# Experts share a job of 128 rows on TensorE's column tiles, and their rows are summed to tokens on chip

## The reference, cut to what matters

```python
def moe_ffn(h, ...):                          # h: (264, 1024)
    ...                                       # sigmoid scores, 4 of 8 groups, top 8 of 64 experts
    gates = jnp.zeros((n, N_EXPERTS)).at[rows, idx].set(w)
    hg = jnp.einsum('nd,edf->nef', h, e_gate)         # e_gate, e_up: (64, 1024, 256)
    hu = jnp.einsum('nd,edf->nef', h, e_up)
    act = jax.nn.silu(hg) * hu * gates[:, :, None]
    routed = jnp.einsum('nef,efd->nd', act, e_down)   # e_down: (64, 256, 1024)
    return routed + shared                            # then x = x + gate2 * this, and a final rmsnorm
```

## Time and profile before

| | |
|---|---|
| median of 3 runs | 1032.44 us (1031.85 to 1032.86) |
| profiled execution, time | 1032.33 us |
| profiled execution, span | 1030.6 us |
| TensorE busy | 935.5 us (91% of the span) |
| VectorE, ScalarE, GpSimd busy | 474.7, 282.3, 174.7 us |
| moved by DMA | 305.58 MB, mean 297 GB/s |
| HBM read, written | 304.78 MB, 26.97 MB |

### The profile page before, as it was taken

The page is one execution under the profiler, slowest core; times in us unless marked ns, Lnnn a source line. Parts: engine busy times, 40 slices in busy tenths (PEclk is TensorE's granted clock), DMA queues, the critical chain, the costliest instruction groups (busy, mean ns, idle before and its releaser), DMA issues.

```text
span 1030.6 us, 18438 instructions
## 1 busy us (share of the span) xinstructions
PE 935.5 (91%) x6425; PEld 653.2 (63%) x6425; DVE 474.7 (46%) x1210; ACT 282.3 (27%) x501; POOL 174.7 (17%) x173
## 2 busy tenths in 40 slices
PE   2799999999998988999998988989989999999980
PEld 1699999999997876445555545545545554555540
DVE  1556899899858443622233223223223322322217
ACT  3544435434373220111212112112111211211232
POOL 2000000000000001022223213213223222322322
PEclk9899999999999969999999999989999999999995
DMA  9975558777766185589999999999999999999922
GB/s 333 266 232 150 181 167 287 245 248 289 240 228 235 54 340 219 188 300 331 359 366 377 396 347 371 367 337 377 392 363 381 402 387 370 391 395 388 373 77 108
DMA packets 103497, 305.58 MB, mean 297 GB/s; under 512 B 13251, under 2 KB 55363, under 8 KB 78452
## 3 DMA queue, kind: packets, MB, share of 16 engines
q1 hardware_dynamic: 89715, 283.80, 73.4%
q0 software_dynamic: 13232, 19.68, 7.9%
q10 hardware_dynamic: 499, 1.40, 0.4%
HBM read 304.78 MB, written 26.97 MB: 322 GB/s over the span
## 4 chain that ended last, share of the span: by engine, by line
PE 63%; DMA 29%; DVE 5%; ACT 1%; issue 1%; SPq 1%; ACTq 0%; DVEq 0%; POOLq 0%
DMA wexp<-in_e_up 27%; PE psum L755 25%; PE psum L1022 14%; PE psum L759 5%; PE psum L1024 4%; PE psum L1050 3%; PE psum L1055 2%; PE psum L774 2%; PE psum L945 2%; DMA bc<-in_norm_g 1%; PE psum L810 1%; PE psum L1025 1%; PE psum L936 1%; PE psum L993 1%; DVE wexp_r L1436 1%
## 5 line engine op out<-in xcount | busy, mean ns | idle before, releaser
L755 PE MATMUL psum<-xn_r,wexp_r 128*128 128x264 f32 x1024 | 192.6, 288 | 2.2 <-DVE wexp_r L1436 2.2
L1024 PE MATMUL psum<-wexp,mid 128*64 128x256 f32 x720 | 173.9, 384 | 0.6 <-DMA wexp<-in_e_up 0.6
L1025 PE MATMUL psum<-wexp,mid 128*64 128x256 f32 x720 | 174.0, 384 | 0.0
L1022 PE MATMUL psum<-wexp,mid 128*128 128x512 f32 x304 | 149.3, 637 | 24.2 <-DMA wexp<-in_e_up 23.4
L755 PEld LDWEIGHTS psum<-xn_r,wexp_r 128*128 128x128 f32 x1024 | 161.0, 191 | 4.9 <-DVE wexp_r L1436 2.7
L1840 DVE SCALAR_TENSOR_TENSOR hT<-psum,gcol,hT 128x256 f32<-128x256 f32 (+1 forms) x64 | 30.6, 478 | 288.0 <-ACT hT L1347 221.3
L755 PE MATMUL psum<-hT_r,wexp_r 128*128 128x264 f32 x512 | 146.0, 285 | 0.0
L1436 DVE TENSOR_TENSOR wexp_r<-wexp,wexp_r 128x1024 fp32r<-128x1024 f32 x88 | 106.4, 1216 | 27.5 <-ACT wexp_r L1189 27.2
L1024 PEld LDWEIGHTS psum<-wexp,mid 128*64 128x64 f32 x720 | 92.3, 136 | 39.2 <-issue 6.1
L1022 PEld LDWEIGHTS psum<-wexp,mid 128*128 128x128 f32 x304 | 58.9, 204 | 86.5 <-issue 85.4
L1189 ACT ACTIVATE wexp_r<-wexp 128x1024 fp32r<-128x1024 f32 x88 | 92.1, 1053 | 49.3 <-PE psum L755 42.5
(11 more groups left out here) (287 smaller groups left out, 1119.4 us busy)
## 6 DMA issues: line engine op xcount, KB each, us to landing
wexp<-in_e_gate SPq DMA_DIRECT2D x64, 1024.0 KB
wexp<-in_e_up SPq DMA_DIRECT2D x64, 1024.0 KB
wexp<-in_e_down SPq DMA_DIRECT2D x64, 1024.0 KB
wexp<-in_w_in SPq DMA_DIRECT2D x32, 1024.0 KB, 6.0
mid<-in_ada_w SPq DMA_DIRECT2D x8, 2048.0 KB, 9.7
wexp<-in_ada_w SPq DMA_DIRECT2D x4, 2048.0 KB, 20.2
wexp<-in_w_branch SPq DMA_DIRECT2D x8, 1024.0 KB, 5.1
wexp<-in_w_out SPq DMA_DIRECT2D x4, 1024.0 KB, 5.8
```

What stands on the lines that cost most here:

```text
L755: last = mm(out, a[x], b[y], start=start and x == y == 0, stop=stop and x == 1)
L1022: last = mm(psum[:, j % 2, :].rearrange("p (a f) -> p a f", a=2), x[:, k, :], w[:, k], start=(k == 0), stop=(k == KT - 1))
L1024: mm(psum[HALF:CAP, j % 2, 0:FE], x[:, k, 0:HALF], w[:, k, 0], start=(k == 0), stop=(k == KT - 1), tile_position=(0, HALF))
L1025: last = mm(psum[0:HALF, j % 2, 0:FE], x[:, k, 0:HALF], w[:, k, 1], start=(k == 0), stop=(k == KT - 1), tile_position=(0, 0))
```

## The change

- Jobs: 33 in place of 64. Body 0 is as before (four jobs, one expert each). Seven bodies follow with eight experts each: jobs 0 and 1 have one expert (up to 128 rows), job 2 two (64 rows each), job 3 four (32 rows each). A last job has four. The rows of a job's experts stand side by side in its 128 rows; `up` and `down` run one product per expert on its column tile (64 or 32 wide), each with 512 columns streaming.
- Rooms: there are still four. Job 0 uses room 0, job 1 room 1, job 2 rooms 2 and 3, job 3 all four, and SyncE's order of loads is written anew.
- Sums: no scatter and no tables in DRAM. `down`'s result is split into a high part (ScalarE) and a low part (VectorE), and two steps later TensorE multiplies a one-hot of tokens (`spread_hot`, 128 rows by 264 tokens) by both parts in five pieces (`sum_piece`): four of 128 tokens x 512 columns in the one-pass format, and one for the 8 samples in f32 on two column tiles. VectorE adds each piece to `y_sum` in SBUF. The pieces stand between the parts of `up`, which is cut in four.
- Gathers take 128 rows for each job. The lists of a shared job are sums over its experts (up to 12 small products). The end of the kernel reads `y_sum` in place of the tables, and VectorE does all of it.

```diff
+BODIES = 7
+LAST = BODIES + 1
+N_JOBS = UNROLL * LAST + 1
+PER_BODY = 8
+SHARE = (1, 1, 2, 4)
+FIRST_PLACE = (0, 1, 2, 4)
+SINGLES = 2 * BODIES
+PAIRED = 2 * BODIES
...
+        y_sum = mod_room[:, 0:2 * D].rearrange("p (t d) -> p t d", t=2)
+        y_sum_samples = mod_room[0:SAMPLE_ROWS, 2 * D:2 * D + BLK]
...
-        y_rows = mT[:, :, :].rearrange("p k t -> p (k t)")[:, 0:2 * D].rearrange("p (b d) -> p b d", b=2)
+        y_high, y_low = [mT[:, :, :].rearrange("p k t -> p (k t)")[:, a * D:(a + 1) * D] for a in range(2)]
...
+        def share_of(i, j):
+
+            if isinstance(i, int) and i in (0, LAST):
+                return 4 if i else 1
+            return SHARE[j]
...
+        def rooms_of(i, j):
+
+            share = share_of(i, j)
+            return [j] if share == 1 else [2, 3] if share == 2 else [0, 1, 2, 3]
+
+        def loads_until(i, j):
+
+            if isinstance(i, int) and i == 0:
+                return 1
+            return 2 * i + (1 if j == 3 else 0)
+
+        def parts_of(i, j):
+
+            n = P // share_of(i, j)
+            return [(q, room, slice(q * n, (q + 1) * n), {} if n == P else {"tile_position": (0, q * n)})
+                    for q, room in enumerate(rooms_of(i, j))]
...
-            def reload(i, s):
-                n = UNROLL * i + s
-                e = expert_of(i, s)
-                sp.wait_ge(S["up_done"], n - 3)
-                load_gate_up(e, s)
-                pi, ps = (i if s else i - 1), (s - 1) % UNROLL
-                if isinstance(pi, int) and pi == 0:
-                    return
-                before = expert_of(pi, ps)
-                sp.wait_ge(S["down_done"], 2 * (n - 4))
-                load_down(before, ps)
...
+            def jobs_before(i, j, room):
+
+                if j == 3:
+                    return UNROLL * i + min(room, 2) + 1
+                if isinstance(i, int) and i == 1:
+                    return room + 1
+                return UNROLL * i
+
+            def gate_up_of(i, j):
+                for place, room in zip(places_of(i, j), rooms_of(i, j)):
+                    e = expert_at(place)
+                    sp.wait_ge(S["up_done"], jobs_before(i, j, room))
+                    load_gate_up(e, room)
+
+            def down_of(i, j):
+                for place, room in zip(places_of(i, j), rooms_of(i, j)):
+                    e = expert_at(place)
+                    sp.wait_ge(S["down_done"], 2 * jobs_before(i, j, room))
+                    load_down(e, room)
+
+            def body(i):
+                gate_up_of(i, 0)
+                if isinstance(i, int) and i == 1:
+                    sp.wait_ge(S["shared_done"], 6)
+                    load_down(1, 1)
+                gate_up_of(i, 1)
+                down_of(i, 0)
+                gate_up_of(i, 2)
+                down_of(i, 1)
+                gate_up_of(i, 3)
+                down_of(i, 2)
+                down_of(i, 3)
...
+            body(1)
+            with sp.Fori(2, LAST) as i:
+                body(i)
+            gate_up_of(LAST, 0)
+            down_of(LAST, 0)
...
-            def scatter(i, j):
-                e = UNROLL * i + j
-                pool.wait_ge(S["scatter_row_ready"], e + 1)
-                need(pool, scattered[j % 2], 16 * (2 * i + j // 2))
-                pool.wait_ge(S["ys_act"], e + 1)
-                pool.wait_ge(S["ys_dve"], e + 1)
...
-                g.indirect_dma_start(out=(y_even, y_odd)[j % 2], out_offset=bass.IndirectOffsetOnAxis(ap=scatter_row[0:n, j, :].bitcast(mybir.dt.uint32), axis=0),
-                                     in_=y_rows[0:n, j % 2, :], in_offset=None,
-                                     bounds_check=last_token, oob_is_err=False, compute_op=ALU.add).then_inc(scattered[j % 2], 16)
...
                 for k in ks:
-                    if is_large(i, j):
-                        last = mm(psum[:, j % 2, :].rearrange("p (a f) -> p a f", a=2), x[:, k, :], w[:, k], start=(k == 0), stop=(k == KT - 1))
-                    else:
-                        mm(psum[HALF:CAP, j % 2, 0:FE], x[:, k, 0:HALF], w[:, k, 0], start=(k == 0), stop=(k == KT - 1), tile_position=(0, HALF))
-                        last = mm(psum[0:HALF, j % 2, 0:FE], x[:, k, 0:HALF], w[:, k, 1], start=(k == 0), stop=(k == KT - 1), tile_position=(0, 0))
+                    for q, room, rows, tile in parts_of(i, j):
+                        last = mm(psum[rows, j % 2, :].rearrange("p (a f) -> p a f", a=2), x[:, k, rows], w_gu[room][:, k],
...
+                need(pe, S["y_lo_rows"], 2 * e)
+                need(pe, S["sum_done"], N_PIECES * e)
...
+                for h in range(2):
+                    for f in range(2):
+                        for q, room, rows, tile in parts_of(i, j):
+                            last = mm(psum[rows, 3 + h, :], a[:, f, rows], w_dn[room][:, f, h * BLK:(h + 1) * BLK],
+                                      start=(f == 0), stop=(f == 1), **tile)
+                    last.then_inc(S["down_done"], 1)
...
+            def sum_piece(hot, m):
+
+                t, h, bank = piece_of(m)
+                t0, n = TILES[t]
+                if t < 2:
+                    for y in (y_high, y_low):
+                        last = mm(psum[:, bank, :], as_r(hot[:, t0:t0 + n]), as_r(y[:, h * BLK:(h + 1) * BLK]), start=(y is y_high), stop=(y is y_low))
+                    return last
+                for y in (y_high, y_low):
+                    for h in range(2):
+                        last = mm(psum[32 * h:32 * h + n, bank, :], as_r(hot[:, t0:t0 + n]).bitcast(F32), as_r(y[:, h * BLK:(h + 1) * BLK]).bitcast(F32),
+                                  start=(y is y_high), stop=(y is y_low), tile_position=(0, 32 * h))
+                return last
+
+            def sums(i, j, pieces):
+
+                e = UNROLL * i + j
+                for m in pieces:
+                    if m == 0:
+                        pe.wait_ge(S["hot_ready"], e + 1)
+                        pe.wait_ge(S["y_lo_rows"], 2 * e + 2)
+                    else:
+                        need(pe, S["sum_done"], N_PIECES * e + m - 1)
+                    sum_piece(spread_hot[:, j % 2], m).then_inc(S["sum_full"], 1)
...
-            def body(i, first=False, last=False):
-                for j in range(UNROLL):
+            def body(i, first=False):
+                for j in steps(i):
                     prev = not (first and j == 0)
                     pi, pj = (i if j else i - 1), (j - 1) % UNROLL
-                    up(i, j, (0, 1, 2, 3))
+                    older = two_before(i, j)
+                    done = not (first and j < 2)
+                    up(i, j, (0, 1))
+                    if done:
+                        sums(*older, (0, 1))
+                    up(i, j, (2, 3))
                     if prev:
                         if first and j == 1:
                             pe.wait_ge(S["job_ready"], 1)
                         turn_act(pi, pj)
                     else:
                         turn_for_sort()
-                    up(i, j, (4, 5, 6, 7))
-                    if not (last and j == UNROLL - 1):
+                    if done:
+                        sums(*older, (2, 3))
+                    up(i, j, (4, 5))
+                    if done:
+                        sums(*older, (4,))
+                    up(i, j, (6, 7))
+                    if not (isinstance(i, int) and i == LAST):
...
-                need(ac, scattered[j % 2], 16 * (2 * i + j // 2))
-                F(y_rows[0:n, j % 2, 0:BLK], psum[CAP - n:CAP, 3, :], ACT.Copy).then_inc(S["ys_act"], 1)
-
+                need(ac, S["sum_full"], N_PIECES * e)
+                for h in range(2):
+                    ac.wait_ge(S["down_done"], 2 * e + h + 1)
+                    F(as_r(y_high[:, h * BLK:(h + 1) * BLK]), psum[:, 3 + h, :], ACT.Copy).then_inc(S["y_hi_rows"], 1)
...
+            def spread_out_rows(i, j):
 
                 e = UNROLL * i + j
                 ve.wait_ge(S["lst_ready"], e + 1)
-                need(ve, scattered[j % 2], 16 * (2 * i + j // 2 - 1))
-                n = rows_used(i, j)
-                V.tensor_copy(scatter_row[0:n, j, :], idx[0:n, j, :]).then_inc(S["scatter_row_ready"], 1)
+                need(ve, S["sum_full"], N_PIECES * (e - 1))
+                if isinstance(e, int) and e == 0:
+                    ve.wait_ge(S["tokens_ready"], 1)
+                V.tensor_scalar(as_r(spread_hot[:, j % 2, :]), token_order, token_of[:, j, :], None, ALU.is_equal).then_inc(S["hot_ready"], 1)
+
+            def add_piece(m, done):
+
+                t, h, bank = piece_of(m)
+                to = y_sum[:, t, h * BLK:(h + 1) * BLK] if t < 2 else y_sum_samples
+                n = P if t < 2 else SAMPLE_ROWS
+                V.tensor_tensor(to, psum[0:n, bank, :], to, ALU.add).then_inc(done, 1)
+
+            def sums_out(i, j):
+
+                e = UNROLL * i + j
+                need(ve, S["sum_done"], N_PIECES * e)
```

(68 more changed lines are left out.)

317 lines of the change are left out of this document (150 added, 167 removed).

## The result

The changed kernel takes 1187.24 us (median of 4 runs, 1182.87 to 1192.56), the one before 1032.65 us beside it (4 runs): a ratio of 1.149, 95% interval 1.145 to 1.153. The forecast was 1148 us in a range of 1110 to 1190, so the sign and the range held. The time is 39 us above the likeliest value and outside the narrower own range of 1125 to 1175. The profiled execution took 1184.55 us for a span of 1182.7.

What follows compares the result with a forecast made beforehand. Waits from SyncE's load order were to bound it, with TensorE idle some 20 us a body. Body 1 ends at 537.1, six bodies of 86.9 reach 1058.5, last quad and tail 1146, plus 1.7: 1148 us; range 1110 to 1190.

Steps and rivals of the forecast that it cites:

- The long wait: Before a body's first up, TensorE idles some 12 us until room 0's gate/up weights land.
- the one before the quad: TensorE waits about 8 us before the quad's up, for gate/up of rooms 2 and 3.
- the first term: From the end of a quad's up to the next body's first up: 4.3 + 3.0 + 2 x 2.44 + 4.9 = 17.0 us.
- first step with the clock: A body's first single: a step of 15.6 us, plus 1.9 us for slow records after the wait.
- second step: A body's second single: 15.6 us, from 11.8 + 1.9 + 1.7 + 0.2, without a wait.
- the pair's `up`: In job 2's step, 11.1 us pass until up is done, 6.9 us of it the up products.
- the quad's loads: After the pair's up, gate/up for rooms 2 and 3 take 3.0 + 9.8, given as 12.7 us.
- its `up` with the clock: In the quad's step, 11.1 us until up is done, plus 1.9 us for slow records after the wait.
- Rival B: Four column tiles run less in parallel, adding 3.1 us per quad's up and 1.5 per down: 1185 us; chance 0.13.
- Rival C: The waits occur but TensorE's clock stays at 2.4 GHz after them, so 15 waits of 1.9 go: 1120 us; chance 0.1.
- Rival A: Loads are covered and TensorE sets the pace, 63.2 us for eight experts: 958 us; chance 0.05.
- the signs: Room 0 refilled every 83 to 90 us, waits of about 12 and 8 us, DMA line at 7, clock line under 9.

Runs made afterwards that it cites:

- e1: Changed kernel with SyncE issuing room 0's gate/up of the next body ahead of the quad's down weights for rooms 2 and 3: 1109.69 us.
- e2: Changed kernel with SyncE issuing the pair's gate/up ahead of the first single's down weights: 1176.67 us.
- e6: Changed kernel with jobs ordered 1, 2, 1, 4 experts, plus the load orders of e1 and e2: 1054.85 us.
- e5: Changed kernel with turn, sums and the quad's down ahead of up in the step that begins with the long wait (TensorE's order alone): 1112.41 us.
- e8: e7 with turn and sums, not down, also ahead of up in the first single's and the quad's steps: 1021.50 us, ratio 0.989 to the kernel before.
- e4: Kernel before the change, each scatter replaced by a plain transfer of 16 numbers, experts' output left out: 998.24 us, ratio 0.967.
- e7: e6 with turn, sums and down of the job before placed ahead of up in the last quad's step: 1049.89 us.
- e10: The kernel of e8 unchanged, run again in more rounds: 1022.52 us, ratio 0.990 to the kernel before.
- e3: Changed kernel with each sum piece covering 16 of its 512 columns on TensorE and VectorE, most experts' output left out: 1131.24 us.

## Why the prediction was right, and where the 39 us come from

**The waits.** The forecast's core, that a quad frees all four rooms at once and TensorE then waits where SyncE's order stops, is shown from both sides: e1, e2 and e6 shorten one wait each by SyncE's order or the order of jobs, e5 by TensorE's, and each gets about its price back, in e1 75.7 us of waiting and 77.5 of time. The long wait was read as some 12 us and is 13.9, the one before the quad as 8 and is 8.2. Their number was short by one: a wait of 1.3 us before the pair was not foreseen. I let the loads for rooms 2 and 3 of the pair "land while job 1 runs (to 48.2)"; they miss it by 1.3 here and by 1.0 to 2.3 in all six bodies.

**The period, term by term** (the body from 741.21 to 832.15, predicted first; the first term stands at its end): from the quad's `up` done to the first `up` 17.0, measured 18.1; first step with the clock 17.5 and 18.1; second step 15.6 and 15.6, then the unforeseen 1.3; the pair's `up` 11.1 and 11.9; the quad's loads 12.7 and 12.8; its `up` with the clock 13.0 and 13.2. The mean body is 91.6 against 86.9, and 4.7 x 6 = 28 us of the 39. Body 1 ended 3.1 us late (540.25 for 537.1). The rest of the way, from the last body's quad to the end of the span, took 93.3 us against 87.6 (1.7 of it before the last `up`), and 2.7 lie between the profiled execution and the median of the runs.

**The first term.** The two largest errors of a body are this term, 18.5 us on the average of six bodies for 17.0, and the unforeseen wait, 1.5 us on the average. Part of the term is the way to the first issue, 4.9 us from the quad's `up` for 4.3. The rest is what follows it: from the issue of the quad's down (727.14) to the first use of room 0 (741.21) 14.1 us pass (13.1 before 558.20, 13.2 before 832.15), where 12.7 stood (3.0 + 9.8). A dearer start of the transfers is not the reason:

```profile
729.20:741.08 11.88, 0.00 (x0) 0.00 (x0) 0.16 (x1) 0.00 (x0) 0.99 (x1) 0.50 1.01 402
```

From 2.1 us after the issue the queues are full, at 402 GB/s. From 727.14 to 741.08 they move 4.99 MB, but room 0's gate/up and the two downs are only 4.2; the others are the gather's and those of room 1's gate/up, which are issued from 731.73 on and share the engines. The sum had room 0's loads alone there. At its own 426 GB/s the 4.99 MB take 11.7 us, so 2.2 us are left for start and end (an estimate; 1.8 in the next body, where 4.81 MB move in 13.08 us). The Trainium skill ("DMA: Bandwidth & Descriptors", Anatomy of one DMA) has a fixed 2.0 us on GpSimd's path, and these loads of SyncE are near it; the lone 1 MB load of the earlier trace rows, with 3.0, is not. The 2.0 us that the prediction read as a value load were in part a wait of SyncE for a `down` (it ends at 836.96, and the load is issued at 837.18): here one issue follows the other by 1.2 us with a value load between them (759.50 to 760.69). No term used them.

**Tiles.** Rival B is out: sixteen records of four tiles take 1.85 us, eight of two tiles 1.87 and four of a whole one 1.72 in the chain above, so four tiles do 3.7 times as much in a microsecond as one (16 / 1.85 over 4 / 1.72). The Trainium skill ("TensorEngine Tiling (Array Packing)", Theoretical Speedup) has up to 4, and the trace agrees with its 3.7. The pair's four parts of `up` take 7.57 us, where 6.9 was set (1.94 + 1.87 + 1.87 + 1.89): 0.7 of the 0.8 us of its term.

**Sums.** In the step shown they take 1.13 + 0.92 + 1.82 = 3.87 us, for 1.9 + 1.7 predicted. With the 0.2 us for changes of tile shape that is what the sum had, and the step without a wait is 15.6 us as it said.

**The clock.** Rival C is out: after the long wait the first four records take 3.77 us where four later take 1.72, and the granted clock over the five bodies is 0.87. In e8 the pauses are at most 1.5 us within a body and the clock stays at 1.00. What the clock alone costs was not separated: the first step is 2.5 us longer than the second (18.1, 15.6), for 1.9 assumed. The last `down` shows it at its strongest:

```profile
1143.93 9.66 DMA wexp<-in_e_down
...
1153.94 6.28 PE psum L1070 x32
```
```profile
1154.00:1160.00 6.00, 6.00 (x32) 1.49 (x32) 0.69 (x1) 0.60 (x1) 0.00 (x0) 0.56 0.00 0
```

Its 32 records took 3.62 us at 755.73 and 6.28 here, after a wait of 7.0 us, at a granted clock of 0.56; 1.9 had been added for it, and 2.7 were due.

**Where the expected gain went.** Rival A's 958 us is not reached by e8 either, in which nearly all waits for gate/up are gone. A body of e8 has 65.0 us of work on TensorE (130.02 / 2), for 63.2 in my sum. Four jobs' sums are 4 x 3.87 = 15.5 of it, so products, turns and lists are 49.5 us, and one expert to a job needs 66.7 (e4): sharing saves 17 us on TensorE for eight experts, and the sums eat 15.5. What is left as a gain is little more than the scatters' time, and in the changed kernel the waits, with the slow records after them, took back all of it and 155 us more. In e8 3 us of each body's 68.2 are spent waiting for VectorE. From the first `up` of body 1 to the step of the last four experts it takes 478.4 us (471.61 to 949.97) where the kernel before takes 504.3 (461.45 to 965.77), 26 less. But body 1 starts 10.2 later, mostly because the two steps before it have sums in them (15.6 for 11.8 us each), and from the start of the last four experts to the end 68.5 us pass for 64.8, with the wait of 13.0 for down weights in them. So 12 us are left of the span.

**How far luck went.** The measured 1187.24 us lie where rival B had its time (1185), but by another way: four tiles are as fast as taken, and the 39 us are small misses of most terms, all to one side. The upper bound of 1190 was taken from B, and without that rival the range would have been too narrow. The mechanism was right; that its number stayed within the range is in part luck. Of the signs, the refill of room 0 comes every 91.6 us, not every 83 to 90; the clock line, the order of the waits and the idle DMA are as said.

**Left open.** In e7 to e10 a wait of 13.0 to 14.4 us is left at the last quad's step, before the `down` that goes ahead of `up`; no order was tried that removes it. The kernel before, without scatters but with one expert to a job and sums on chip, was not run.

## What to carry to other kernels

When jobs share buffers, count how many buffers one job frees at once and what stands behind each wait in an in-order queue of loads: one job that takes every buffer empties the queue once per cycle, however low the mean loads of engines and DMA are. Free as many of its buffers as you can before the job ahead of it (e6), load first what is needed first (e1), and put work that is already ready into the wait (e5, e8). Cost the sum of what replaces a slow path too: here the sums use up nearly all that sharing saves.

## What the runs showed of the hardware that I had not expected

A product with 16 streaming columns in place of 512 saves only half of its time in the one-pass format. In body 1's pair step, where neither kernel had waited and the granted clock is 1.00, four such records take:

```profile
502.43 1.21 PE L1080 MATMUL psum<-mT_r,hT_r 128*128 128x512 f32 x4
```
```profile
493.28 0.61 PE L1081 MATMUL psum<-mT_r,hT_r 128*128 128x16 f32 x4
```

The four behind the turn go from 1.17 to 0.59, so the place makes no difference, and the eight f32 records of the samples' piece, whose stationary side has 8 columns and not 128, from 1.89 to 0.26; the 0.77 us of e3 above were measured at a granted clock of 0.71. Four column tiles of 32 with 512 columns run nearly four at a time (3.7). And a wait of 7.0 us before 32 records that can't be overlapped costs 2.7 us more in the records themselves (6.28 for 3.62).
